# The rope's turn moved behind the norm on VectorE, and the squares of 32 heads split between ScalarE and GpSimd for fp32r sums

## The reference: what is computed

```python
# branch A: 128 plain + 64 rotated dimensions
qn = _rmsnorm(qa[..., :A_NOPE], a_g_q[:A_NOPE])
qr = _rope(_rmsnorm(qa[..., A_NOPE:], a_g_q[A_NOPE:]), *rope_a)
kn = _rmsnorm(kva[..., :A_NOPE], a_g_k[:A_NOPE])
# branch B: two halves of 64 dimensions, the first 16 of each rotated
bq = _partial_rope(_rmsnorm(b_q.reshape(b, s, B_HEADS, 2, B_DK), b_g_q), *rope_b)
bk = _partial_rope(_rmsnorm(b_k.reshape(b, s, B_HEADS, 2, B_DK), b_g_k), *rope_b)
# branch C: no rotation, a bias per head
cq = _rmsnorm(c_q.reshape(b, s, C_HEADS, C_DH), c_g_q)
ck = _rmsnorm(c_k.reshape(b, s, C_HEADS, C_DH), c_g_k)
```

## Time and profile before

| | us |
|---|---|
| median of 3 runs | 3438.83 (3438.08 to 3439.68) |
| the profiled execution | 3443.66 |
| its span, first to last instruction | 3441.9 |
| TensorE busy | 3373.0 (98%) |
| VectorE busy | 2160.6 (63%) |
| ScalarE busy | 1706.2 (50%) |
| GpSimd busy | 199.2 (6%) |
| TensorE's granted clock | 0.999 of full speed |

### The profile page before, as it was taken

How to read it: one execution, slowest core, us unless ns; L and a number is a source line. 1 busy time by engine, 2 the same in 40 slices (tenths; PEclk the granted TensorE clock), 3 DMA queues, 4 the chain that set the end, 5 groups by cost and what they waited for, 6 DMA issues and landing times. The chain is left out here.

```text
span 3441.9 us, 73246 instructions
## 1 busy us (share of the span) xinstructions
PE 3373.0 (98%) x27922; PEld 3306.5 (96%) x27922; DVE 2160.6 (63%) x3598; ACT 1706.2 (50%) x2796; POOL 199.2 (6%) x217
## 2 busy tenths in 40 slices
PE   8999999999999999999999999999999999999999
PEld 7999999999999999899999999999889999999999
DVE  7677666556656666677655565565667755566565
ACT  5555544434434455655545554445655554554443
POOL 1100100000000024000000000001000000010000
PEclk9999999999999999999999999999999999999999
DMA  5324555555555554344454445554344355444554
GB/s 192 108 99 167 173 177 189 188 179 189 189 183 183 187 182 150 138 147 145 163 195 178 171 162 185 182 201 174 132 147 147 135 185 200 176 160 180 182 198 167
DMA packets 90612, 584.04 MB, mean 170 GB/s; under 512 B 10480, under 2 KB 11120, under 8 KB 28400
## 3 DMA queue, kind: packets, MB, share of 16 engines
q1 hardware_dynamic: 88992, 577.47, 47.5%
q0 software_dynamic: 1488, 4.72, 0.4%
HBM read 580.05 MB, written 2.10 MB: 169 GB/s over the span
## 5 line engine op out<-in xcount | busy, mean ns | idle before, releaser
L191 PE MATMUL bank<-h,w_hi 128*128 128x256 f32 x5728 | 1633.2, 285 | 17.2 <-DVE w_lo L172 11.0
L172 DVE TENSOR_TENSOR w_lo<-raw,w_hi 128x768 fp32r<-128x768 f32 (+5 forms) x1202 | 1348.1, 1131 | 475.9 <-ACT w_hi L161 471.1
L193 PE MATMUL bank<-h,w_lo 128*128 128x256 f32 x5728 | 1604.0, 280 | 0.0
L192 PE MATMUL bank<-h,w_hi 128*128 128x256 f32 x5728 | 1600.8, 279 | 0.0
L161 ACT ACTIVATE w_hi<-raw 128x768 fp32r<-128x768 f32 (+4 forms) x1190 | 1093.9, 967 | 236.6 <-PE bank L193 210.6
L191 PEld LDWEIGHTS bank<-h,w_hi 128*128 128x128 f32 x5728 | 1079.7, 188 | 33.5 <-issue 11.1
L192 PEld LDWEIGHTS bank<-h,w_hi 128*128 128x128 f32 x5728 | 1080.4, 189 | 3.7 <-issue 2.4
L193 PEld LDWEIGHTS bank<-h,w_lo 128*128 128x128 f32 x5728 | 1079.4, 188 | 0.0
L191 PE MATMUL bank<-mixed,w_hi 128*128 128x256 f32 x2304 | 646.0, 280 | 0.7 <-DVE w_lo L172 0.7
L193 PE MATMUL bank<-mixed,w_lo 128*128 128x256 f32 x2304 | 644.3, 280 | 0.0
L192 PE MATMUL bank<-mixed,w_hi 128*128 128x256 f32 x2304 | 642.3, 279 | 0.0
(11 more groups left out here) (378 smaller groups left out, 2778.2 us busy)
## 6 DMA issues: line engine op xcount, KB each, us to landing
raw<-in_w SPq DMA_DIRECT2D x485, 1024.0 KB, 4.8
raw<-in_w_br SPq DMA_DIRECT2D x96, 512.0 KB, 4.2
raw<-in_w_uq SPq DMA_DIRECT2D x8, 768.0 KB, 4.4
raw<-in_w_ukv SPq DMA_DIRECT2D x8, 512.0 KB, 3.2
bias_t<-in_bias POOLq DMA_DIRECT2D x16, 192.0 KB, 3.2
x<-in_x SPq DMA_DIRECT2D x4, 512.0 KB, 7.9
raw<-in_w_kr SPq DMA_DIRECT2D x4, 512.0 KB, 3.3
out_x<-x SPq DMA_DIRECT2D x3, 512.0 KB, 7.6
```

The lines of the kernel that those rows point to most:

```text
L172: dve.tensor_tensor(w_lo[:, b % 2, c], raw[:, b, c], w_hi[:, b % 2, c].bitcast(F32), ALU.subtract).then_inc(S["lo_done"], 1)
L191: pe.matmul(o, w_hi[:, b % 2, c], a_hi, start=start and k == t0, stop=False)
L192: pe.matmul(o, w_hi[:, b % 2, c], a_lo, start=False, stop=False)
L193: last = pe.matmul(o, w_lo[:, b % 2, c], a_hi, start=False, stop=stop and k == t0 + nt - 1)
```

## The change

Two edits are made together.

The turn: in B, `rotate` runs at b = 0 right behind the norm, no longer at b = 1. In A, `pair_rope` is cut in two: the shuffle and the two products with sine and cosine (now `pair_turn`) run at the end of the pair's own body, and only the two additions stay behind the norm.

The squares, in the 16 B and 16 C heads: ScalarE writes its squares as fp32r into a new buffer `sq_hi`. GpSimd squares the same rows in fp32 into `sq` and subtracts, into fp32r `sq_lo`. TensorE sums `sq_hi` and `sq_lo` in two fp32r matmuls of 512 columns with an fp32r copy of the ones, in place of one fp32 matmul. GpSimd's gate of a head now comes after the next head's squares in its program, and a copy of the ones is made once at the start.

```diff
+                def low_squares(T, part, row, at):
+
+                    pool.wait_ge(S["h_ss"], T)
+                    for k in range(2):
+                        pool.wait_ge(S[f"bank{k}"], at)
+                        src = pre[:, row + 3 * k, :]
+                        pool.tensor_tensor(sq[:, k, :], src, src, ALU.mult).then_inc(S["sq_full"], 1)
+                    pool.wait_ge(S["sq_full"], 2 * part + 2)
+                    pool.wait_ge(S["h_sq"], 2 * T + 2)
+                    pool.tensor_tensor(sq_lo[:, :, :], sq, sq_hi[:, :, :].bitcast(F32), ALU.subtract).then_inc(S["sq_lo"], 1)
...
-                with pool.Fori(0, NH) as i:
-                    gated(head_no(l, BR_B, i), 0, head_no(l, BR_B, i))
...
+                head_squares(BR_B, 0)
+                with pool.Fori(1, NH) as i:
+                    head_squares(BR_B, i)
+                    head_gate(BR_B, i - 1)
+                head_gate(BR_B, NH - 1)
...
+                head_squares(BR_C, 0)
+                band_bias(0)
+                with pool.Fori(1, NH) as i:
+                    head_squares(BR_C, i)
+                    head_gate(BR_C, i - 1)
+                    band_bias(i)
+                head_gate(BR_C, NH - 1)
...
-                        squares(T, b, pre[:, 3 * b, :])
+                        squares(T, b, pre[:, 3 * b, :], sq_hi)
...
-            def pair_rope(pair):
-                dve.wait_ge(S["qk_zero"], 1)
+            def pair_turn(pair):
+
                 dve.wait_ge(S["qr_n"], pair + 1)
                 dve.memset(stat[:, 3, 2:3], 0.0)
                 dve.stream_shuffle(rope[:, 1, :], rope[:, 0, :], A_PARTNERS).then_inc(S["qr_rot"], 1)
                 dve.wait_ge(S["qr_rot"], pair + 1)
                 dve.tensor_tensor(rope[:, 1, :], rope[:, 1, :], sin_a, ALU.mult).then_inc(S["qr_s"], 1)
                 dve.tensor_tensor(rope[:, 0, :], rope[:, 0, :], cos_a, ALU.mult).then_inc(S["qr_s"], 1)
+
+            def pair_rope(pair):
+                dve.wait_ge(S["qk_zero"], 1)
                 dve.wait_ge(S["qr_s"], 2 * pair + 2)
...
                     z_one(T, 0)
-                elif k == 1:
                     if br == BR_B:
                         rotate(T, B)
+                elif k == 1:
+                    return
...
+                pe.matmul(m[0][:, :], sums_r[:, at:at + P], sq_hi[:, :, :].rearrange("p k s -> p (k s)"), start=True, stop=False)
+                pe.wait_ge(S["sq_lo"], part + 1)
+                pe.matmul(m[0][:, :], sums_r[:, at:at + P], sq_lo[:, :, :].rearrange("p k s -> p (k s)"), start=False,
+                          stop=True).then_inc(S["h_ss"], 1)
```

More of the change, by code:

```diff
@@ L1512, in hybrid_layers @@
         g[k] for k in ("load_unit", "split_hi", "split_lo", "split_lo_part", "unit", "unit_tiles", "of"))
-    x, h, ident, ones, ones64, eps = (g[k] for k in ("x", "h", "ident", "ones", "ones64", "eps"))
+    x, h, ident, ones, ones64, eps, shared = (g[k] for k in ("x", "h", "ident", "ones", "ones64", "eps", "shared"))
     bank, m, sqx, tn, rn, mid = (g[k] for k in ("bank", "m", "sqx", "tn", "rn", "mixed"))
@@ L1542, in hybrid_layers @@
         sq, rs = sqx[:, 0, :].rearrange("p (k s) -> p k s", k=2), sqx[:, 1, :].rearrange("p (k s) -> p k s", k=2)
+        sq_hi = buf("sq_hi", [2, SEQ], F32R)
+        sq_lo = buf("sq_lo", [2, SEQ], F32R)
+        sums_r = buf("sums_r", 2 * P, F32R)
         rope = tn[:, 0, :].rearrange("p (k s) -> p k s", k=2)
@@ L1582, in v_no, with split_no @@
             return l * (2 * NH + NH // 2) + (0, NH // 2, NH // 2 + NH)[br] + i
+        def split_no(l, br, i):
+            return l * 2 * NH + (br - BR_B) * NH + i
         def b_no(l, hd):
@@ L1705, in _ @@
         def _(pool):
+            pool.tensor_copy(sums_r[:, :], shared[:, P:3 * P]).then_inc(S["sums_r"], 1)
             pool.memset(qk[:, 0:2, :], 0.0).then_inc(S["qk_zero"], 1)
@@ L1718, in _ @@
             for l in range(NL):
+                n0 = base(l)
                 def latent_add(k, src, count):
@@ L1735, in gated, with head_squares, head_gate @@
                     pool.tensor_tensor(zs[:, e, :], pre[:, 7 + e, :], sig[:, e, :], ALU.mult).then_inc(S["z_silu"], 1)
+                def low_squares(T, part, row, at):
[7 more added lines that the diff above has]
+                    pool.tensor_tensor(sq_lo[:, :, :], sq, sq_hi[:, :, :].bitcast(F32), ALU.subtract).then_inc(S["sq_lo"], 1)
+                def head_squares(br, i):
+                    at = 2 * (n0 + (L_B, L_C)[br - BR_B] + i - N_FIRST) + 1
+                    low_squares(head_no(l, br, i), split_no(l, br, i), 0, at)
+                def head_gate(br, i):
+                    gated(head_no(l, br, i), 0, head_no(l, br, i))
                 with pool.Fori(0, NH // 2) as i:
@@ L1741, in _, with band_bias @@
                         gated(T, e, T if e == 0 else T - 1)
-                with pool.Fori(0, NH) as i:
-                    gated(head_no(l, BR_B, i), 0, head_no(l, BR_B, i))
-                with pool.Fori(0, NH) as i:
+                head_squares(BR_B, 0)
[3 more added lines that the diff above has]
+                head_gate(BR_B, NH - 1)
+                def band_bias(i):
                     pool.wait_ge(S["max0"], 2 * head_no(l, BR_C, i))
@@ L1777, in z_sigmoid, with squares @@
                 act.activation(sig[:, e, :], sig[:, e, :], ACT.Exp, scale=-1.0).then_inc(S["z_sig"], 1)
-            def squares(T, k, src):
+            def squares(T, k, src, dst):
                 act.wait_ge(S["h_ss"], T)
-                act.activation(sq[:, k, :], src, ACT.Square).then_inc(S["h_sq"], 1)
+                act.activation(dst[:, k, :], src, ACT.Square).then_inc(S["h_sq"], 1)
             def norm(br, T, B=None):
@@ L1833, in pair_hooks @@
                         act.wait_ge(S[f"bank{b}"], 2 * (base(l) - N_FIRST) + 2 * (L_A + j) + 2)
-                    squares(T + 1, 0, pre[:, 1, :])
-                    squares(T + 1, 1, pre[:, 4, :])
+                    squares(T + 1, 0, pre[:, 1, :], sq)
+                    squares(T + 1, 1, pre[:, 4, :], sq)
                 elif k == 1:
@@ L1892, in pair_body @@
                         act.activation(osq, m[1][:, 0:SEQ], ACT.Square).then_inc(S["qr_sq"], 1)
-                        squares(T, 0, bank[0][:, 0:SEQ])
+                        squares(T, 0, bank[0][:, 0:SEQ], sq)
                         act.activation(pre[:, 0:2, :], bank[0][:, :].rearrange("p (k s) -> p k s", k=2), ACT.Copy).then_inc(S["bank0"], 1)
                     else:
-                        squares(T, 1, bank[1][:, 0:SEQ])
+                        squares(T, 1, bank[1][:, 0:SEQ], sq)
                         act.wait_ge(S["v_tr"], v_no(l, BR_A, i))
@@ L2179, in pair_body @@
                         dve.scalar_tensor_tensor(rope[:, 0, :], pre[:, 2, :], gq[:, 1:2], ors, ALU.mult, ALU.mult).then_inc(S["qr_n"], 1)
+                        pair_turn(pair)
                     if b < 2:
@@ L2341, in free, with norm @@
                 pe.wait_ge(S[f"bank{b % 2}"], 2 * (n - N_FIRST) + b // 2)
-            def norm(T, sums=ones):
+            def norm(T, part=None, at=0):
                 pe.wait_ge(S["h_sq"], 2 * T + 2)
                 pe.wait_ge(S["h_ln"], T)
-                pe.matmul(m[0][:, :], sums, sq.rearrange("p k s -> p (k s)"), start=True, stop=True).then_inc(S["h_ss"], 1)
+                if part is None:
+                    pe.matmul(m[0][:, :], ones, sq.rearrange("p k s -> p (k s)"), start=True, stop=True).then_inc(S["h_ss"], 1)
+                    return
+                pe.wait_ge(S["sums_r"], 1)
+                pe.matmul(m[0][:, :], sums_r[:, at:at + P], sq_hi[:, :, :].rearrange("p k s -> p (k s)"), start=True, stop=False)
+                pe.wait_ge(S["sq_lo"], part + 1)
+                pe.matmul(m[0][:, :], sums_r[:, at:at + P], sq_lo[:, :, :].rearrange("p k s -> p (k s)"), start=False,
+                          stop=True).then_inc(S["h_ss"], 1)
             def score(br, T, B, e):
@@ L2416, in head_hooks @@
                     pe.wait_ge(S["v_tok"], v_no(l, br, j))
-                    norm(T, ones if br == BR_C else ones64)
+                    norm(T, split_no(l, br, j), 0 if br == BR_C else P)
                 elif k == 2:
```

1 line of the change is left out of this document (removed).

## The result

The changed kernel takes 3419.48 us (median of 5 runs, 3417.29 to 3424.91) against 3438.83 in the same job. Its profiled execution took 3417.29, with a span of 3415.2. The runs of a kernel fall into two groups some 7 us apart (of before, over all jobs, 3436 to 3440 and 3442 to 3447; of after 3417 to 3421 and 3425), and the profiled execution of before is of its upper group. That stretch goes from 1751.60 to 1732.27, 19.3 us less.

The account below looks back on a forecast made before the run. TensorE, busy 98% of the span, was taken to bound the kernel, with VectorE's loop next in B. Gains of 6.5 (C), 6.0 (B) and 5.7 us (A), 18.2 together, gave 3420.6 from 3438.8; range 3400 to 3431.

Parts of the forecast that it names:

- Steady B: B heads after a layer's first two: VectorE's loop of 26.90 us plus 0.8 gives 27.7, gaining 0.17 to 0.2 each.
- the blocking: In B, GpSimd's subtraction holds up VectorE's w_lo parts behind unit 1: 0.8 us a head, bounds 0 and 2.8.
- three rows that the prediction draws on: Trace cases of VectorE slowed beside GpSimd: L2042 0.96 us against 0.48, L2085 1.11 against 0.55, w_lo pair 2.79 against 2.38.
- Rival 1: No blocking by GpSimd: B's period 26.90 us, 0.97 gained per steady head, total 3408.6; chance 0.18.
- TensorE's own time in B: TensorE's side of a B body: 27.87 us less 1.31 of wait and 0.41 of sum, 26.15.
- The first two B heads: Start of each layer's B: having slack, the first head gains 1.65 us and the second 0.4.
- A: A's turn cut in two: 1.1, 1.15 and 0.6 us gained, 2.85 per layer, 5.7 in both.
- C: C's 16 heads: the shorter TensorE sum gains 0.41 us each within 1.5 of slack, 6.5 in all.
- 2: Rival: all 28.4 us of turn waits go and 32 heads gain 0.41 each, 3397 us; chance 0.05.
- 3: Rival: the subtraction slips behind VectorE's first w_lo part and blocks the second, 1.1 to 1.5 us a head, 3428; chance 0.16.
- 5: Rival: all 2.8 us a head of GpSimd's work fall on VectorE's loop, slower at 3459 us; chance 0.03.
- 4: Rival: fp32r sums of 512 columns cost as much as fp32, only C's 6.5 us are lost, 3427; chance 0.08.

Follow-up runs that it names:

- t_only: The changed kernel with the turn's move kept and the squares put back as before (fp32, no new GpSimd work): 3418.14 us.
- defer2: The changed kernel, with GpSimd's subtraction waiting until VectorE has negated the previous head's maxima: 3408.02 us.
- defer: The changed kernel, with GpSimd's subtraction waiting until VectorE has done both parts of unit 3's w_lo: 3420.17 us.
- first_c: best_all with B's sums in fp32 again and the split squares in C alone: 3395.05 us.
- s_only: The changed kernel with the split squares kept and the turn put back where it was: 3434.09 us.
- comb_fix: The changed kernel, with the turn of each layer's last B head one unit later, as before the change: 3417.65 us.
- a_adds: The changed kernel, with A's two additions also moved to the end of the pair's own body: 3411.08 us.
- best_all: The changed kernel with the edits of a_adds, comb_fix and defer2, and in B unit 0 taken from its bank before the turn: 3398.29 us.

## Why the prediction was right, and where not

*That it gains, and where the wait goes: right.* The wait for B's turn went and came back as one for the probabilities (L2131), 1.24 us a head as forecast.

*Steady B: 27.7 forecast, 27.3 measured.* Its loop without blocking, 26.90, is 26.78 in t_only and 26.80 in defer2. (By the prediction's own steps, 3.40 less 2.40, it would be 26.87.) The term most mis-sized is the blocking: 0.8 was taken and 0.50 is due. The place was right: the subtraction ended 2.55 us behind unit 1's start (2.65 forecast, with squares of 0.61 for the 0.74 taken), on the first part of `w_lo`. That part then ended 0.82 us behind the subtraction, less than its own 0.96: the two together make the second part 0.50 late instead of 0.75. Of the three rows that the prediction draws on, L2085 is a TENSOR_SCALAR with one tensor input, as the sign change in defer is: more is held up than instructions with two tensors. Rival 1 was right on the loop and wrong on the blocking, which exists.

*TensorE's own time in B, 26.15 with the short sum: 25.90.* The step took the 1.31 us of idle as the wait's cost. From the start of the matmul before to that of the first score it takes 1.59 us in before and 0.11 in first_c, so the wait costs 1.48, and the eight score matmuls behind it take 0.10 longer (1.41 for 1.31). Together that is 1.58: the fp32 kernel's own body is 27.87 - 1.58 = 26.29, as first_c ran. The error did nothing to the forecast, where VectorE's loop decides, but it spoiled the expectation for first_c.

*The first two B heads: 2.05 forecast per layer, 2.1 measured* (1.12 + 1.01 in the first layer).

*B in all: 3.0 per layer forecast, 5.0 measured*, the difference being the five steady heads, at 0.55 to 0.64 each where 0.17 to 0.2 stood: three parts in four of it the smaller blocking (0.3 us), the rest the loop (0.1).

*The first comb body: forecast 0, measured 1.5 and 1.1 lost.* The prediction weighed the turn against unit 0 only in bodies with a B head behind them. The last head's turn lies in a comb body, where VectorE went from a wait of 2.19 us into a chain without slack. t_only has the loss (+1.5), s_only hardly (+0.3), comb_fix takes it away.

*A: 2.85 per layer forecast, 1.9 measured.* The failed step is "the additions then follow L2042 and end where TensorE is ready: the wait goes". The step set them at their unblocked 0.87 us and charged the gate only to unit 0. They took 1.40, 0.5 of the 0.6 us that the scores still wait. a_adds, where they meet no gate, shows them at 0.87 and gains 3.1 more per layer. Three pairs gave 0.78 each, where 1.1, 1.15 and 1.3 stood. The last step of A's stretch, in B's first bodies, lost 0.42 (0.7 forecast); it loses the same in s_only and 0.02 in t_only, so the squares do it, as the prediction had it.

*C: 0.41 a head forecast, 0.45 measured.* The sum itself gives 0.39 (0.86 - 0.47). Another 0.06 lies in the 48 products behind the transposition (5.68 us for 5.74). These 0.06 are not the sum's own: in some layers, the first of defer among them, the products take 5.74 with the fp32r sums too, and the bodies 24.81. Why they differ stays open.

So two misses of the prediction, A and the comb body (together +4.5 us), were paid by B, which gave 4.2 beyond its forecast outside the place where before's trace was slow. That the total came so near is luck in part: its terms are further off.

*Rivals.* 2 (all cover kept, 3397) is no limit: first_c and best_all reach 3395 and 3398 once unit 0 no longer waits for the turn and the subtraction meets nothing. 3 and 5 are out: the price is 0.5. 4 is out: 512 fp32r columns go in 0.24.

## What to carry to other kernels

When an instruction moves, follow it through every body in which its code runs, the last and the first of a loop above all: the turn's move alone (t_only) gained 1.1 us in a steady B body and lost 1.2 to 1.5 in the first body of the next kind. GpSimd's work is cheap by its place, not by its length: one 1.3 us subtraction cost 0.5 us a head beside weights, 0.6 beside an operation of two columns, and nothing where VectorE waited. Before shortening work on an engine, make the chain that bounds it short enough: in B the fp32r sums lost 0.5 us a head at first, and gained 0.1 only after the turn stood behind the eviction.

## What the runs showed of the hardware

A wait of TensorE can cost more than itself, and not each time. Before, twice at the same place of a layer, windows of 2 us behind the wait (us, busy times, then the granted clock):

```profile
1469.00:1471.00 2.00, 2.00 (x17) 1.90 (x16) 0.78 (x2) 1.79 (x3) 0.00 (x0) 1.00 0.24 98
...
2549.00:2551.00 2.00, 1.66 (x6) 1.51 (x7) 0.86 (x3) 1.11 (x3) 0.00 (x0) 0.56 0.48 201
2551.00:2553.00 2.00, 2.00 (x10) 1.82 (x10) 1.72 (x2) 1.47 (x3) 0.00 (x0) 0.58 0.00 0
```

And the scores that waited:

```profile
1468.65 1.55 PE L2359 MATMUL m<-qk 128*128 128x128 f32 x8 [2.12 <-DVE qk L2056]
...
2549.34 2.90 PE L2359 MATMUL m<-qk 128*128 128x128 f32 x8 [2.18 <-DVE qk L2056]
```

After 2.12 us of idle the granted clock stayed at its upper level (2.4 GHz). After 2.18 it was mostly at the lower (1.2 GHz) for some 3 us, and that head took 37.00 us against 35.51 in before's second trace. comb_fix met the same once, in a head that took 28.3 us for the usual 26.9, after a wait of 1.94 us. The wait's length does not decide it: after waited 1.93 us at the same place, and s_only 2.17 at both places of before, and the clock stayed up. So one trace of a kernel can carry such a 1.5 us, which is no effect of the edit.

A VectorE instruction that GpSimd holds up ends sooner behind GpSimd's than its own length, by 0.14 us in three places: the first part of `w_lo` in after 0.82 of 0.96 us, the first of A's two additions there 0.28 of 0.42, the sign change in defer 0.03 of 0.17.

The stretch ahead of the hybrid layers took 1347.9 to 1350.3 us in nine traces and 1355.9 to 1357.3 in three: both of before, and best_all, which differs from first_c only in the hybrid layers. From 700 to 900 us TensorE made 1700 matmuls in before's trace and 1717 in after's, at a granted clock of 1.00 in both: a pace 1% lower, which the clock doesn't show. Its cause stays open.
